# Biases by ScalarE's queue in pieces, once-filled slots for a later expert's down rows, and a reordered start and end of an expert loop

## The chip, the cores and the metric

One core of a Trainium2 chip runs one program. The metric is device time in microseconds of one launch, median of the runs shown. The engines are TensorE (PE), VectorE (DVE), ScalarE (ACT), GpSimd (POOL) and SyncE (SP), which here issues every DMA. Sixteen DMA engines serve the core. Everything is float32.

## What is computed

Two blocks in sequence on 256 tokens of width 1024. The first (two layers of feed-forward, gated mixers, feed-forward) is not touched. The second is an attention layer followed by a mixture of 32 experts, of which each token takes 4:

```python
def moe_ffn(h, w_router, b_router, w_gate_up, b_gate_up, w_down, b_down):
    logits = (h @ w_router).astype(jnp.float32) + b_router.astype(jnp.float32)
    top_val, top_idx = lax.top_k(logits, TOP_K)
    gates = jax.nn.softmax(top_val, axis=-1)
    ...
    def expert_block(args):
        xe, e = args
        gu = xe @ w_gate_up[e] + b_gate_up[e]
        g = jnp.minimum(gu[:, :D_FF_2], SWIGLU_LIMIT)
        u = jnp.clip(gu[:, D_FF_2:], -SWIGLU_LIMIT, SWIGLU_LIMIT)
        act = (u + 1.0) * (g * jax.nn.sigmoid(SWIGLU_ALPHA * g))
        return act @ w_down[e] + b_down[e]
    ...
# the layer returns x + gate2 * y, y the gated sum over a token's experts
```

Per expert, `w_gate_up[e]` is 1024x2048 (8 MB) and `w_down[e]` 1024x1024 (4 MB), so the 32 experts read 384 MB.

## The kernel before

`attend_phase` ends with the router; `experts_phase` follows it and does for each expert at most 64 tokens (CAP). More than 64 would go to `late_experts`, which doesn't run on these inputs.

**Tiles and slots.** An expert has 8 gate-up tiles of 128x2048 and 4 down tiles that hold 256 rows of `w_down`, each 1 MB and one DMA. All loads have a number in order of use: `number(e, j)`. Expert 0's gate-up is 0 to 7; then each turn e has 12: gate-up of e (j = 0 to 7) and the down rows of e - 1 (j = 8 to 11). Numbers run through a cycle of 12 slots (6 of `chip.ring`, 6 of `room.more`). Besides there are EXTRA = 4 slots that are filled once (`room.once`), in words that become free when attention is done. Before, they hold the numbers 12 to 15, that is gate-up tiles 4 to 7 of expert 1. Loads 0 to 11 and those four are in flight or landed when the experts start, the last two issued at the start of `experts_phase`.

**SP** (`turn(e)` of the sync block) issues first the row of biases of e (`bias_row`, 8 KB into one partition, waits until the row before has been broadcast), then the loads. Each load waits on `chip.used`, which PE raises when it has read the tile that was in the slot (`emptied`). All these DMAs stand in SP's one queue.

**POOL** (`spread_bias`) broadcasts the row to 128 partitions when it has landed and when `activate(e - 1)` has read the one before (`gu_read`). A small addition (L2616) stands before the broadcast (L2617).

**PE**, per turn: `gate_up(e)` (L2637; after its fourth tile `turn_back`, L2663, two transposes), `gather(e)` (L2672, picks the tokens of e + 1), `down(e)` (L2653), `turn_hidden(e)` (L2682, transposes), `scatter(e)` (L2692, four products of 64 rows that add the expert's output into four PSUM banks that hold the whole result). Turn 0 has gate-up and gather, then four products with `b_down` (L2719, 32 rows), which set the banks, then `turn_hidden(0)`. Turn 1 is written out, and only it has `add_x` (L2699), which adds x through the identity. Turns 2 to 31 are a loop.

**ACT**, per turn: `take_back` (L2735), `take_gathered` (L2740), `sigmoid` (L2744), `take_hidden` (L2748). **DVE**: selections, `activate` (L2790 to L2806), `take_down` (L2812). At the end ACT copies token block 0 (L2762) and DVE token block 1 (L2835) from PSUM, both after the whole last scatter, and SP stores both (L2500).

Of the kernel before, what the change touches and what calls it, by code (L numbers as in the profile page):

```python
# [11 lines left out]
P = 128  # L12
RING = 6
EXTRA = 4
# [1596 lines left out]

def attend_loads(chip, w_in, w_out):
# [56 lines left out]
def attend_phase(chip, s, spent, routed, room, par, loads, base, n_project, b_down, mod_row, w_gate_up, rows_before):  # L1669
# [26 lines left out]
    with nc.Block() as block:  # L1696
        @block.sync
        def _(sp):
# [29 lines left out]
            for i in range(EXTRA - 1):  # L1728
                sp.dma_start(room.once[i], gate_up_rows(w_gate_up, *divmod(2 * RING + i, KD))).then_inc(chip.once[i], 16)
# [420 lines left out]
        def _(dve):  # L2150
# [290 lines left out]
CAP = 64  # L2441
ACC, GATE_BANK, UP_BANK, Y_BANK, SHARED_BANK = 0, 4, 5, 6, 7
EXPERTS = ("e_bias_row e_bias gu_read g_ready sig gated hidden sel back back_turned back_out gathered xe "
           "turned act ye scat down_bias tables first_rows last_rows")
# [16 lines left out]
LATE_WORDS = 2048 + 256 + 1 + 4 * 1024 + 256 + NE + 1 + 6 * SLOT + P  # L2461
# [19 lines left out]
class LateRoom:  # L2481


    def __init__(self, chip, words):
# [7 lines left out]
        self.places = w.take(P)  # L2492
# [5 lines left out]
def store(chip, sp, routed, out, tt, done):  # L2498

    sp.dma_start(out[0:1, tt * P:tt * P + P, :].rearrange("b p d -> (b p) d"), routed.acc[:, tt, :]).then_inc(done, 16)  # L2500


def experts_phase(chip, s, spent, base, routed, room, gatesT, b_down, w_gate_up, b_gate_up, w_down, out):
# [16 lines left out]

    def once(e, j):

        return number(e, j) - CYCLE if isinstance(e, int) and CYCLE <= number(e, j) < CYCLE + EXTRA else None

    def in_cycle(e, j):

        if isinstance(e, int):
            n = number(e, j)
            turn, p = divmod(n if n < CYCLE else n - EXTRA, CYCLE)
# [26 lines left out]
    def emptied(e, j):  # L2556
# [3 lines left out]
        n = number(e, j) - EXTRA - CYCLE  # L2560
        return base + (n if n < CYCLE else n + EXTRA) + 1
# [3 lines left out]
    with nc.Block() as block:  # L2565
        @block.sync
        def _(sp):
            def bias_row(e):
                reach(sp, s["e_bias"], e)
                sp.dma_start(room.bias_row[0:1, :],  # L2570
                             b_gate_up[0:1, ds1(e), :].rearrange("a e n -> (a e) n")).then_inc(s["e_bias_row"], 16)

            def down_rows(e, k):
                return w_down[0:1, ds1(e), 2 * k * P:2 * k * P + 2 * P, :].rearrange("a e (c p) n -> p (a e c) n", p=P)

            def load(e, j, src):

                if not isinstance(e, int) or number(e, j) >= CYCLE + EXTRA:
# [26 lines left out]
            sp.wait_ge(s["first_rows"], 1)  # L2605
            store(chip, sp, routed, out, 0, chip.stored)
            sp.wait_ge(s["last_rows"], 1)
# [17 lines left out]
        def _(pe):  # L2625
            mm = nc.tensor.matmul

            def gate_up(e, between=None):

                pe.wait_ge(s["xe"], e + 1)  # L2630
                reach(pe, s["gu_read"], e)
                for k in range(G8):
# [53 lines left out]
            def scatter(e):  # L2686
# [15 lines left out]
            def turn(e):  # L2702
                gate_up(e, lambda: turn_back(e))
# [3 lines left out]
                if isinstance(e, int):  # L2707
                    add_x()
                scatter(e)
# [360 lines left out]
```

## Time and profile before

| | us |
|---|---|
| runs: median of 3 (lowest, highest) | 2349.98 (2349.85, 2355.32) |
| the profiled execution | 2348.43 |
| its span, first to last instruction | 2346.8 |
| PE busy | 2238.3 (95%) |
| DVE busy | 1027.9 (44%) |
| ACT busy | 597.7 (25%) |
| POOL busy | 169.7 (7%) |
| experts_phase, about | 1374 to 2346.8 |

The profile is one execution. Its times count from the first instruction. A busy PE isn't PE at its peak: matmuls are pipelined. "DMA share" is the mean busy share of the 16 DMA engines; transfers of one engine overlap a little, so a full stream is shown slightly above 1. PEclk is the granted clock of TensorE as a part of full speed.

### The profile page before, as it was taken

To read this page: it belongs to the slowest core of one execution; us is meant where nothing else is said; L and a number is where in the kernel's file an instruction comes from. 1 tells how busy PE (TensorE), PEld (TensorE's weight loads), DVE (VectorE), ACT (ScalarE), POOL (GpSimd) and SP (SyncE) were. 2 spreads that over 40 slices of the span, in tenths; PEclk is the share of its full clock that TensorE was granted. 3 is DMA by queue.
4 is the path that set the end of the run, shared out by engine and by line. 5 is a ranking of instruction groups with operands and counts; after the bars stand their busy time and mean duration, and the time that the engine had idled before them with its cause. 6 is when DMAs were issued, how large, how long until landed. Compare 5 with 4: busy or idle time off the path is not lost. (4 is left out here: it accounts for less than half of the span.)

```text
span 2346.8 us, 32064 instructions
## 1 busy us (share of the span) xinstructions
PE 2238.3 (95%) x12797; PEld 1401.5 (60%) x12798; DVE 1027.9 (44%) x1492; ACT 597.7 (25%) x808; POOL 169.7 (7%) x194
## 2 busy tenths in 40 slices
PE   7999989999999999999999999999999999999998
PEld 6886875788788777668877554444333333333333
DVE  4563583665565457456658642222222222212221
ACT  4432331543443232243436510000000000000000
POOL 5000020000000002000000001000000000000000
PEclk9999999999999999999999999999999999999999
DMA  8763311686386342168635568999999999999996
GB/s 285 240 245 105 122 60 59 213 285 234 122 282 241 104 162 73 38 199 278 213 133 171 211 264 344 416 418 418 418 418 418 418 418 418 418 418 418 418 418 270
DMA packets 231966, 633.58 MB, mean 270 GB/s; under 512 B 32480, under 2 KB 128752, under 8 KB 199072
## 3 DMA queue, kind: packets, MB, share of 16 engines
q1 hardware_dynamic: 231872, 632.24, 71.2%
q8 instruction: 70, 1.15, 0.2%
q14 instruction: 24, 0.20, 0.0%
HBM read 631.12 MB, written 1.07 MB: 269 GB/s over the span
## 5 line engine op out<-in xcount | busy, mean ns | idle before, releaser
L403 PE MATMUL banks<-ffn_room 128*128 128x512 f32 x1920 | 453.7, 392 | 0.0
L403 PEld LDWEIGHTS banks<-ffn_room 128*128 128x128 f32 x1920 | 357.6, 188 | 72.6
L520 DVE TENSOR_TENSOR ffn_room<-memory,ffn_room 128x2048 fp32r<-128x2048 f32 x124 | 280.9, 2292 | 98.6 <-ACT ffn_room L480 98.6
L2790 DVE TENSOR_TENSOR attend_words<-banks,memory 64x512 f32<-64x512 f32 x64 | 44.2, 690 | 550.4 <-PE banks L2637 550.0
L480 ACT CAST ffn_room<-memory 128x2048 fp32r<-128x2048 f32 x124 | 232.0, 1903 | 68.4 <-PE banks L421 61.8
L421 PE MATMUL banks<-ffn_room 128*128 128x512 f32 x1056 | 248.2, 390 | 0.3
L2637 PE MATMUL banks<-attend_later,attend_words 128*64 128x512 f32 x1000 | 232.7, 600 | 14.7 <-DMA attend_later<-in_w_gate_up 12.2
L2653 PE MATMUL banks<-memory,attend_words 128*64 128x512 f32 x1008 | 223.5, 595 | 0.0
L421 PEld LDWEIGHTS banks<-ffn_room 128*128 128x128 f32 x1056 | 197.7, 188 | 42.7 <-DVE ffn_room L559 2.1
L2637 PE MATMUL banks<-memory,attend_words 128*64 128x512 f32 x776 | 179.9, 599 | 13.1 <-DMA memory<-in_w_gate_up 12.4
L2637 PEld LDWEIGHTS banks<-attend_later,attend_words 128*64 128x64 f32 x1000 | 66.8, 137 | 154.8 <-issue 102.4
L2653 PEld LDWEIGHTS banks<-memory,attend_words 128*64 128x64 f32 x1008 | 69.0, 136 | 128.6 <-issue 119.8
L2672 PEld LDWEIGHTS banks<-attend_words,memory 128*128 128x128 f32 x1056 | 120.5, 192 | 26.0 <-issue 26.0
L2637 PEld LDWEIGHTS banks<-memory,attend_words 128*64 128x64 f32 x776 | 50.6, 136 | 136.6 <-issue 103.1
L2672 PE MATMUL banks<-attend_words,memory 128*128 128x64 f32 x1056 | 124.8, 277 | 0.0
L2740 ACT COPY attend_words<-banks 128x512 f32<-128x512 f32 x33 | 19.4, 587 | 401.1 <-PE banks L2672 401.1
L486 ACT ACTIVATE memory<-banks 128x256 f32<-128x256 f32 x88 | 33.8, 385 | 341.5 <-PE banks L403 319.5
L535 DVE TENSOR_TENSOR memory<-memory,banks 128x256 f32<-128x256 f32 x88 | 36.8, 418 | 175.4 <-ACT memory L486 164.2
L869 PE MATMUL banks<-memory 128*128 128x400 f32 (+1 forms) x256 | 101.1, 549 | 1.2 <-PEq L363 1.2
L2617 POOL PARTITION_BROADCAST memory<-attend_words x32 | 73.7, 2304 | 267.3 <-issue 267.3
L2812 DVE TENSOR_TENSOR attend_words<-banks,kept 128x512 f32<-128x512 f32 x32 | 22.2, 693 | 147.2 <-PE banks L2653 147.2
L865 PE MATMUL banks<-memory 128*128 128x256 f32 x384 | 85.4, 379 | 0.0
(430 smaller groups left out, 2328.9 us busy)
## 6 DMA issues: line engine op xcount, KB each, us to landing
memory<-in_ffn_w SPq DMA_DIRECT2D x132, 1024.0 KB, 7.3
memory<-in_w_down SPq DMA_DIRECT2D x126, 1024.0 KB, 24.6
attend_later<-in_w_gate_up SPq DMA_DIRECT2D x125, 1024.0 KB, 20.7
memory<-in_w_gate_up SPq DMA_DIRECT2D x97, 1024.0 KB, 17.8
attend_words<-in_w_gate_up SPq DMA_DIRECT2D x33, 1024.0 KB, 23.7
memory<-in_w_in SPq DMA_DIRECT2D x32, 1024.0 KB, 6.0
memory<-in_w_ada SPq DMA_DIRECT2D x32, 768.0 KB, 5.3
memory<-in_w_out SPq DMA_DIRECT2D x12, 1024.0 KB, 4.9
```

The costliest lines, as they stand in the source:

```text
L403: m = nc.tensor.matmul(psum[:, GU + tt, :], x_parts[:, xp, k, tt * P:tt * P + P], rows, start=(n == 0), stop=(n == 3 * KD - 1))
L421: return nc.tensor.matmul(psum[:, 2 * tt + h, :], hidden_parts[:, ft % 2, hp, tt, c, :], rows[:, c, h * 512:h * 512 + 512], start=(ft == 0 ...
L480: nc.scalar.copy(split_place(i)[0], chip.ring[:, chip.slot(base + i), :]).then_inc(s["lead"], 1)
L520: tt_op(b, chip.ring[:, chip.slot(base + i), :], a.bitcast(F32), ALU.subtract).then_inc(chip.used, 1)
L535: tt_op(hidden[:, tt, :], gate[:, tt, :], psum[:, GU + tt, FT:2 * FT], ALU.mult)\
L865: m = mm(psum[:, n % 2, c * 256:c * 256 + 256], slots[k // 4][:, k % 4, cc:cc + P], chip.xT[:, k, :], start=(k == 0), stop=(k == KD - 1))
L869: m = mm(psum[:, n % 2, 0:cols], chip.xT[:, k, half * P:half * P + P], slots[k // 4][:, k % 4, :], start=(k == 0), stop=(k == KD - 1))
L2617: nc.gpsimd.partition_broadcast(room.bias, room.bias_row[0:1, :]).then_inc(s["e_bias"], 1)
L2637: m = mm(psum[halves[h], bank, :], room.xeT[:, k, :], rows[:, c0 + h * HALF:c0 + h * HALF + HALF], start=(k == 0), stop=(k == G8 - 1))
L2653: m = mm(psum[halves[h], Y_BANK, :], room.actT[:, k, :], rows[:, c * D_EXPERT + h * HALF:c * D_EXPERT + h * HALF + HALF], start=(k == 0), ...
L2672: m = mm(psum[:, SHARED_BANK, k * CAP:k * CAP + CAP], routed.h2[:, tt, k * P:k * P + P], room.sel[:, tt, :], start=(tt == 0), stop=(tt == ...
L2790: m = tt_op(room.gate[halves[h], :], psum[halves[h], GATE_BANK, :], room.bias[halves[h], h * HALF:h * HALF + HALF], ALU.add)
```

## The change

1. SP issues no rows of biases. ACT does, from its own queue, as a pattern of 16 pieces of 512 B, row e + 1 between `take_back(e)` and `take_gathered(e)`.
2. The once-filled slots hold the numbers 40 to 43 (`APART` = 3), the down rows of expert 2, read in turn 3. Numbers 12 to 39 go through the cycle of 12. Turns 1 to 3 are written out, since the numbering is irregular there.
3. Turn 0 takes the first two gate-up tiles of expert 1 (`AHEAD`) before `turn_hidden(0)`; turn 1 begins with the third. The products with x and with `b_down` stand together before turn 8 (`QUIET`); scatter(1) sets the banks.
4. The last scatter signals after token block 0. ACT and DVE each copy one half of a block, and the store of block 0 can be issued before block 1 is copied.
5. The late rounds are a loop of two instead of being written twice (left out below but for its head).

```diff
-EXTRA = 4
+EXTRA, APART = 4, 3
...
+def down_pair(w_down, e, k):
+
+    return w_down[0:1, ds1(e), 2 * k * P:2 * k * P + 2 * P, :].rearrange("a e (c p) n -> p (a e c) n", p=P)
...
             sp.wait_ge(s["pv"], ALL)
             for i in range(EXTRA - 1):
-                sp.dma_start(room.once[i], gate_up_rows(w_gate_up, *divmod(2 * RING + i, KD))).then_inc(chip.once[i], 16)
+                sp.dma_start(room.once[i].rearrange("p (c n) -> p c n", c=2), down_pair(w_down, APART - 1, i)).then_inc(chip.once[i], 16)
...
+BIAS_PIECES = 16
+AHEAD = 2
...
+    apart = number(APART, G8)
+
     def once(e, j):
 
-        return number(e, j) - CYCLE if isinstance(e, int) and CYCLE <= number(e, j) < CYCLE + EXTRA else None
+        return number(e, j) - apart if isinstance(e, int) and apart <= number(e, j) < apart + EXTRA else None
...
-        n = number(e, j) - EXTRA - CYCLE
-        return base + (n if n < CYCLE else n + EXTRA) + 1
+        n = number(e, j) - CYCLE
+        if n + CYCLE >= apart:
+            n -= EXTRA
+        return base + (n if n < apart else n + EXTRA) + 1
...
-                if not isinstance(e, int) or number(e, j) >= CYCLE + EXTRA:
+                if not isinstance(e, int) or number(e, j) >= CYCLE:
                     sp.wait_ge(chip.used, emptied(e, j))
...
             def turn(e):
-                late = isinstance(e, int) and e == 2
-                if not late:
-                    bias_row(e)
-                for k in range(G8 if isinstance(e, int) and e == 1 else 0, G8):
+                for k in range(D4 if isinstance(e, int) and e == 1 else 0, G8):
                     load(e, k, gate_up_rows(w_gate_up, e, k))
-                if late:
-                    bias_row(e)
+                if isinstance(e, int) and e == APART:
+                    return
                 for k in range(D4):
                     load(e, G8 + k, down_rows(e - 1, k))
 
-            bias_row(0)
-            for n in (CYCLE - 1, CYCLE + EXTRA - 1):
-                load(1, n - G8, gate_up_rows(w_gate_up, 1, n - G8))
-            turn(1)
-            turn(2)
-            with sp.Fori(3, NE) as e:
+            load(1, D4 - 1, gate_up_rows(w_gate_up, 1, D4 - 1))
+            sp.dma_start(room.once[EXTRA - 1].rearrange("p (c n) -> p c n", c=2), down_rows(APART - 1, EXTRA - 1))\
+                .then_inc(chip.once[EXTRA - 1], 16)
+            for e in range(1, APART + 2):
+                turn(e)
+            with sp.Fori(APART + 2, NE) as e:
                 turn(e)
...
-            def scatter(e):
+            def scatter(e, first=False):
...
-                               start=False, stop=True, skip_group_check=True)
+                               start=first, stop=True, skip_group_check=True)
+                    if tt == 0 and isinstance(e, int) and e == NE:
+                        m.then_inc(s["scat_first"], 1)
                 m.then_inc(s["scat"], 1)
 
-            def add_x():
+            def add_x_and_bias():
+                pe.wait_ge(s["down_bias"], 1)
                 for tt in range(NT):
                     for h in range(2):
-                        mm(psum[:, ACC + 2 * tt + h, :], ident, chip.x[:, tt, h * 512:h * 512 + 512],
-                           start=False, stop=True, skip_group_check=True)
+                        c = slice(h * 512, h * 512 + 512)
+                        for rows, cols in ((ident, chip.x[:, tt, c]), (gatesT[0:NE, tt * P:tt * P + P], b_down[0:NE, c])):
+                            mm(psum[:, ACC + 2 * tt + h, :], rows, cols, start=False, stop=True, skip_group_check=True)
 
             def turn(e):
-                gate_up(e, lambda: turn_back(e))
+                gate_up(e, range(AHEAD if isinstance(e, int) and e == 1 else 0, G8), lambda: turn_back(e))
                 gather(e)
                 down(e, G8)
                 turn_hidden(e)
-                if isinstance(e, int):
-                    add_x()
-                scatter(e)
+                scatter(e, isinstance(e, int) and e == 1)
...
             gather(0)
-            pe.wait_ge(s["down_bias"], 1)
-            for tt in range(NT):
-                for h in range(2):
-                    c = slice(h * 512, h * 512 + 512)
-                    mm(psum[:, ACC + 2 * tt + h, :], gatesT[0:NE, tt * P:tt * P + P], b_down[0:NE, c], start=True, stop=True)
+            gate_up(1, range(AHEAD))
             turn_hidden(0)
-            turn(1)
-            with pe.Fori(2, NE) as e:
+            for e in range(1, APART + 1):
+                turn(e)
+            with pe.Fori(APART + 1, QUIET) as e:
+                turn(e)
+            add_x_and_bias()
+            with pe.Fori(QUIET, NE) as e:
                 turn(e)
...
+            def bias_row(e):
+                reach(act, s["e_bias"], e)
+                act.dma_start(room.bias_row[0:1, :].rearrange("p (a n) -> p a n", a=BIAS_PIECES),
+                              b_gate_up[0:1, ds1(e), :].rearrange("a e (k n) -> (a e) k n", k=BIAS_PIECES))\
+                    .then_inc(s["e_bias_row"], 16)
...
+            bias_row(0)
             take_gathered(-1)
+            bias_row(1)
             take_gathered(0)
             sigmoid(0)
             take_hidden(0)
-            with act.Fori(1, NE) as e:
+            with act.Fori(1, NE - 1) as e:
                 take_back(e)
+                bias_row(e + 1)
                 take_gathered(e)
...
             take_back(NE)
+            act.wait_ge(s["scat_first"], 1)
+            copy(routed.acc[:, 0, 0:512], psum[:, 0, :]).then_inc(s["first_rows"], 1)
             act.wait_ge(s["scat"], NE)
-            copy(routed.acc[:, 0, :], psum[:, 0:2, :].rearrange("p b n -> p (b n)")).then_inc(s["first_rows"], 1)
+            copy(routed.acc[:, 1, 0:512], psum[:, 2, :]).then_inc(s["last_rows"], 1)
...
-                for first_place in (CAP, CAP + P):
-                    late_round(chip, s, routed, room, w_gate_up, b_gate_up, w_down, e, first_place, gate2_row, out)
+                with nc.Fori(0, 2) as half:
+                    late_round(chip, s, routed, room, w_gate_up, b_gate_up, w_down, e, half, gate2_row, out)
```

DVE's two last copies change in the same way, to the halves 512 to 1024 of blocks 0 and 1.

## Rows read from the trace of the kernel before

**Rows 1.** The page, slices of 58.7 us: busy tenths of the 16 DMA engines.

```profile
DMA  8763311686386342168635568999999999999996
```

**Rows 2.** Timeline of POOL: start, duration (us), engine, line, operation, idle before and releaser.

```profile
1481.03 0.35 POOL L2616 TENSOR_TENSOR attend_words<-memory 128x1 f32<-128x1 f32 x1 [16.30 <-DVE attend_words L2795]
...
1564.80 0.35 POOL L2616 TENSOR_TENSOR attend_words<-memory 128x1 f32<-128x1 f32 x1 [16.70 <-DVE attend_words L2795]
...
1623.60 0.19 POOL L2616 TENSOR_TENSOR attend_words<-memory 128x1 f32<-128x1 f32 x1 [19.64 <-DMA attend_words<-in_b_gate_up]
...
2293.36 0.19 POOL L2616 TENSOR_TENSOR attend_words<-memory 128x1 f32<-128x1 f32 x1 [19.54 <-DMA attend_words<-in_b_gate_up]
```

**Rows 3.** Timeline of PE, last gate-up tiles of two late turns.

```profile
1732.24 1.94 PE L2637 MATMUL banks<-attend_words 128*64 128x512 f32 x8 [0.55 <-DMA attend_words<-in_w_gate_up]
1734.73 1.94 PE L2637 MATMUL banks<-memory,attend_words 128*64 128x512 f32 x8 [0.56 <-DMA memory<-in_w_gate_up]
...
2313.22 1.94 PE L2637 MATMUL banks<-memory,attend_words 128*64 128x512 f32 x8 [0.56 <-DMA memory<-in_w_gate_up]
```

**Rows 4.** Timeline of SP's issues, turns 0 to 2 (L2583 loads, L2570 biases).

```profile
1386.74 2.13 SPq L2583 DMA_DIRECT2D memory<-in_w_down  x4
...
1411.67 0.29 SPq L2570 DMA_DIRECT2D attend_words<-in_b_gate_up  x1
1424.26 5.52 SPq L2583 DMA_DIRECT2D memory<-in_w_down  x4
1430.85 0.27 SPq L2570 DMA_DIRECT2D attend_words<-in_b_gate_up  x1
```

**Rows 5.** Waits of SP, 1370 to 1450 us: total, times, longest.

```profile
SPq L2570 <- POOL memory L2617: 12.3, 2, 11.6
```

**Rows 6.** Timeline of PE, turns 0 and 1 (eight records are a gate-up tile).

```profile
1379.06 10.53 PE L2637 MATMUL banks<-memory,attend_words 128*64 128x512 f32 x48 [0.68 <-ACT attend_words L2740]
...
1396.67 5.53 PE L2719 MATMUL banks<-attend_later,attend_words 32*128 32x512 f32 x8
...
1418.57 3.79 PE L2672 MATMUL banks<-attend_words,memory 128*128 128x64 f32 x32
...
1429.80 3.61 PE L2699 MATMUL banks<-memory 128*128 128x512 f32 x8
```

**Rows 7.** Windows: length, busy (count) of PE, PEld, DVE, ACT, POOL; PEclk, DMA share, GB/s.

```profile
1392.00:1416.00 24.00, 24.00 (x106) 10.60 (x104) 5.87 (x12) 3.47 (x5) 2.65 (x2) 0.86 1.02 415
1416.00:1440.00 24.00, 24.00 (x120) 10.59 (x118) 6.80 (x13) 1.71 (x3) 2.66 (x2) 1.00 0.64 242
...
1398.00:1405.00 7.00, 7.00 (x16) 2.49 (x16) 2.34 (x6) 1.89 (x3) 0.00 (x0) 0.53 1.02 424
```

**Rows 8.** Windows at the end of the stream, same columns.

```profile
2322.00:2324.00 2.00, 2.00 (x12) 0.57 (x9) 0.00 (x0) 0.00 (x0) 0.00 (x0) 1.00 0.57 227
2324.00:2326.00 2.00, 2.00 (x12) 0.61 (x9) 0.06 (x1) 0.00 (x0) 0.00 (x0) 1.00 0.08 33
...
2332.00:2334.00 2.00, 2.00 (x12) 0.71 (x10) 0.00 (x0) 0.00 (x0) 0.00 (x0) 1.00 0.03 12
```

**Rows 9.** The page, DMA queues: packets, MB, share of 16 engines.

```profile
q8 instruction: 70, 1.15, 0.2%
```

**Rows 10.** Timeline of all engines in turn 31.

```profile
2302.84 2.30 POOL L2617 PARTITION_BROADCAST memory<-attend_words  x1 [9.28 <-issue]
...
2305.83 0.37 ACT L2735 COPY attend_words<-banks 128x256 f32<-128x256 f32 x1 [9.06 <-PE banks L2663]
```

**Rows 11.** Timeline of all engines at the end.

```profile
2336.11 0.69 DVE L2812 TENSOR_TENSOR attend_words<-banks,kept 128x512 f32<-128x512 f32 x1 [8.97 <-PE banks L2653]
...
2336.86 1.99 PE L2692 MATMUL banks<-attend_words 64*128 64x512 f32 x8 [0.80 <-DVE attend_words L2812]
...
2338.89 1.01 ACT L2762 COPY kept<-banks 128x1024 f32<-128x1024 f32 x1 [9.44 <-PE banks L2692]
2338.89 1.23 DVE L2835 COPY kept<-banks 128x1024 f32<-128x1024 f32 x1 [2.09 <-PE banks L2692]
2339.93 0.83 SPq L2500 DMA_DIRECT2D out<-kept  x2
```

More of the change, by code:

```diff
@@ L1666, with attend_phase @@
 PIECES = ((0, P), (P, WIDE))
-def attend_phase(chip, s, spent, routed, room, par, loads, base, n_project, b_down, mod_row, w_gate_up, rows_before):
+def attend_phase(chip, s, spent, routed, room, par, loads, base, n_project, b_down, mod_row, w_gate_up, w_down, rows_before):
     nc, D, KD, NT = chip.nc, chip.D, chip.KD, chip.NT
@@ L2491, in __init__ @@
         self.selT = w.take(256).rearrange("p (t n) -> p t n", t=2)
-        self.places = w.take(P)
+        self.places = w.take(2 * P).rearrange("p (a n) -> p a n", a=2)
         self.xeT, self.actT = chip.xT[:, :, 0:P], chip.xT[:, :, P:2 * P]
@@ L2528, in in_cycle @@
             n = number(e, j)
-            turn, p = divmod(n if n < CYCLE else n - EXTRA, CYCLE)
+            turn, p = divmod(n if n < apart else n - EXTRA, CYCLE)
             return p, 0, turn
@@ L2626, in _, with gate_up @@
             mm = nc.tensor.matmul
-            def gate_up(e, between=None):
+            def gate_up(e, tiles, between=None):
                 pe.wait_ge(s["xe"], e + 1)
                 reach(pe, s["gu_read"], e)
-                for k in range(G8):
+                for k in tiles:
                     pe.wait_ge(full(e, k), filled(e, k))
@@ L2759, in _ @@
                 take_hidden(e)
+            take_back(LAST)
+            take_gathered(LAST)
+            sigmoid(LAST)
+            take_hidden(LAST)
             take_back(NE)
+            act.wait_ge(s["scat_first"], 1)
+            copy(routed.acc[:, 0, 0:512], psum[:, 0, :]).then_inc(s["first_rows"], 1)
             act.wait_ge(s["scat"], NE)
-            copy(routed.acc[:, 0, :], psum[:, 0:2, :].rearrange("p b n -> p (b n)")).then_inc(s["first_rows"], 1)
+            copy(routed.acc[:, 1, 0:512], psum[:, 2, :]).then_inc(s["last_rows"], 1)
         @block.vector
@@ L2833, in _, with late_round @@
             take_down(NE, taken(NE, D4))
+            dve.wait_ge(s["scat_first"], 1)
+            nc.vector.tensor_copy(routed.acc[:, 0, 512:1024], psum[:, 1, :]).then_inc(s["first_rows"], 1)
             dve.wait_ge(s["scat"], NE)
-            nc.vector.tensor_copy(routed.acc[:, 1, :], psum[:, 2:4, :].rearrange("p b n -> p (b n)")).then_inc(s["last_rows"], 1)
+            nc.vector.tensor_copy(routed.acc[:, 1, 512:1024], psum[:, 3, :]).then_inc(s["last_rows"], 1)
 LATE = ("chain l_gate l_added l_stored l_sel l_gathered l_xeT l_bias_row l_bias l_rows l_gu l_summed l_capped l_sig l_gated l_hidden l_turned "
         "l_actT l_down l_ye l_selT l_scat")
-def late_round(chip, s, routed, room, w_gate_up, b_gate_up, w_down, e, first_place, gate2_row, out):
+def late_round(chip, s, routed, room, w_gate_up, b_gate_up, w_down, e, half, gate2_row, out):
     nc, D, KD, NT = chip.nc, chip.D, chip.KD, chip.NT
@@ L2932, in _ @@
             chain = Chain(dve, s["chain"])
-            chain(ts(room.places, routed.iota, float(first_place), None, ALU.add))
+            for i in range(2):
+                chain(ts(room.places[:, i, :], routed.iota, float(CAP + i * P), None, ALU.add))
             for tt in range(NT):
-                m = ts(room.sel[:, tt, :], room.places, routed.place[:, tt, ds1(e)],
+                m = ts(room.sel[:, tt, :], room.places[:, ds1(half), :].rearrange("p a n -> p (a n)"), routed.place[:, tt, ds1(e)],
                        routed.chosen[:, tt, ds1(e)], ALU.is_equal, ALU.mult)
@@ L2982, in second_half @@
             room = AttendRoom(chip, parts, later, words, routed)
-            attend_phase(chip, s_attend, s_first.span(), routed, room, par, loads, base, n_project, b_down, mod_row, w_gate_up, rows_before)
+            attend_phase(chip, s_attend, s_first.span(), routed, room, par, loads, base, n_project, b_down, mod_row, w_gate_up, w_down, rows_before)
             experts_phase(chip, s_first, s_late.span(), base + n_project + N_OUT, routed, ExpertRoom(chip, words, room), room.gatesT, room.b_down,
```

18 lines of the change are left out of this document (7 added, 11 removed).

## The prediction, made before the changed kernel ran

> **What bounds the kernel now.** I read the page's slices first: from slice 25 on, some 1410 us to the end, the DMA row stands at 9 without a break [rows 1]. That stretch is the 32 experts, 12 loads of 1 MB each. PE is about as busy, so the next view must tell which of the two sets the pace.
>
> The timeline of POOL has one mark per expert: the small addition in front of the broadcast, released when `activate` has read the banks. Between 1481.03 and 1564.80 the mark comes three times in 83.77 us, 27.9 us a turn; between 1623.60 and 2293.36 it comes 22 times in 669.76 us, 30.44 us a turn [rows 2]. PE's timeline says why: in the second stretch the last gate-up tiles start 2.49 us apart and each has waited for a DMA, against 10.53 / 6 = 1.75 us a tile where nothing is awaited [rows 3, 6]. So PE needs 27.9 us a turn and DMA 30.4. PE eats up the lead of 16 loads, and from about 1600 us it runs at DMA's pace. From the mark at 1564.80 to the one at 2293.36 are 24 turns; at 27.92 each the latter would stand at 2234.9. PE has 58 us to spare, and what DMA gains up to that amount is gained at the end.
>
> So the end is: when the stream starts, plus its work, plus its idle time, plus the tail behind the last gate-up tile. Each has a row.
>
> **Start.** SP issues the first load of the long stream at 1386.74 [rows 4], right behind the row of biases of expert 1, for which it had waited up to 11.6 us on the broadcast of row 0, at L2570 [rows 5]. Yet that load's slot was free when PE had done tile 0: 1379.06 + 1.75 = 1380.8 [rows 6].
>
> **Idle.** In 1416 to 1440 the DMA share is 0.64 where a full stream shows 1.02 [rows 7]: 0.38 x 24 = 9.1 us of idle. The reason is in the order: loads 12 to 15 (expert 1, tiles 4 to 7) lie in the once-filled slots and free nothing, so between tile 11 and the first down tile of expert 0 no slot comes free, and SP, which issued a row of biases at 1411.67, issues its next load at 1424.26 [rows 4].
>
> **One engine late.** At the end the share falls to 0.57 in 2322 to 2324, then stands at 0.08, 33 GB/s, and ends in 2332 to 2334 with 0.03 [rows 8]. 1/16 is 0.0625: one DMA engine works on alone. Fifteen stop at 2322 + 2 x (0.57 - 0.06) / (1.02 - 0.06) = 2323.1, the last near 2333.0, 9.9 us later. A load counts as landed with its slowest engine, so PE has been paced by that one. What it has more of is the 8 KB row of biases: 31 in the stream. A tile is 1 MB over 16 engines in 2.49 us, so 8 KB on a single one cost 2.49 / 8 = 0.31 us.
>
> **The change, part by part.** Expert turns are 30.44 = 8 x 2.49 + 0.31 + 4 down tiles, so a down tile is 2.55.
>
> (1) *Rows by ScalarE, in 16 pieces of 512 B.* SP no longer waits for a broadcast: the stream starts at 1380.8, **5.9 us** earlier. In the stream the row leaves the late engine. Two of the 31 rows (experts 2 and 3, issued 1411.67 and 1430.85) fall into idle time and cost nothing now; 29 x 0.31 = 9.0 us are on the path, which the 9.9 us of lag bear out. The 16 pieces aren't free: no row shows 512 B packets between those of another queue. From below they cost 8 KB / 16, 0.02 us on each engine; from above, the instruction queue gives 70 packets of 16 KB at 0.2% of 16 engines, 1.07 us each against 0.62 by the loads' pace [rows 9], so 0.45 us for a packet of another queue. I take 0.05, near the bytes, because the instruction packets partly hit cold engines: 29 x 0.26 = **7.5 us**. ScalarE's issue sits between `take_back` and `take_gathered`. It waits for the broadcast of e; that ends at 2302.84 + 2.30 = 2305.14 and the copy of `take_back` starts at 2305.83 [rows 10], and the next gather, whose result ScalarE copies, comes only behind the last gate-up tile of 2313.22 [rows 3], some 9 us later. Behind the waiting issue are the gathered copy, the sigmoid and the hidden copy; with 9 us of cover this is worth nothing. Without cover every microsecond would be PE's, which has 2.5 a turn.
>
> The Trainium skill, "DMA: Bandwidth & Descriptors", section "Why a DMA increments its semaphore by 16 and not by 1", says that a DMA of SP or ACT runs on the largest k up to 16 that divides the slowest dimension of both patterns, on the lowest-numbered engines, and that a contiguous row sprays if software splits it; the trace agrees that one engine carries the row and that it is the same one each time (9.9 us of lag could not add up otherwise). The same page, "Issuing engines are not separate DMA queues", speaks against half of this part: another issuing engine saves only sequencer time. By that rule the queue alone would be worth the 5.9 us of SP's wait and the splitting the rest.
>
> (2) *Once-filled slots for expert 2's down rows.* The number of loads behind the start stays: 16 lie there beforehand, and up to the last gate-up tile 360 follow. Four are now gate-up instead of down: -0.2 us. What changes is the releases: each of tiles 0 to 39 frees a slot at once. I follow both clocks. DMA, from 1381.9 (data start about 1 us behind the issue), has done 8 loads by 1402; load 20 needs tile 8 read, and with (3) that is 1399.2. It has done 8 more by 1422; load 28 needs tile 16 read: 1418.2. Load 32: DMA 1432, slot 1427.5. Load 44 (slot of 28): DMA 1452, slot 1446. Margins are 1.6 us or more after that 1 us, so the idle time goes: **9.1 us**.
>
> (3) *Two tiles of expert 1 in turn 0, and `add_x` and the bias product moved to turn 8.* The 8 matmuls of 32 rows at L2719 took 5.53 us in turn 0, half of it at a granted clock of 0.5, that is 1.2 GHz instead of 2.4, and `add_x` at L2699 3.6 us in turn 1 [rows 6, 7]. By themselves they save nothing at the end, PE not being the bound; they are the margins of (2): without the two tiles, tile 8 would wait for the sigmoid and its slot would be free about 3.5 us later, an idle time of 2. In turn 8 the same 16 matmuls cost PE 7 to 9 us once, hidden by its 58.
>
> (4) *Last sum by token block.* The eight records of `scatter` take 1.99 us from 2336.86, then ACT copies 1.01 and DVE 1.23 us, and SP issues at 2339.93 [rows 11]. After: block 0 is copied in halves of 512 columns (0.69 us for 128x512 on DVE [rows 11], ACT no longer) from 2337.9 on and stored under the rest; block 1 is out at 2338.9 + 0.7 = 2339.6 instead of 2340.3. Gain 0.6 (copies alone) to 1.3 (the first store's transfer too); I take **0.9**.
>
> Late rounds don't run; their new loop costs nothing. Three unrolled turns instead of one mean more cold code on PE; turn 1, unrolled today, shows no stall.
>
> **Sum.** 5.9 + 7.5 + 0.2 + 9.1 + 0.9 = 23.6. The profiled execution took 2348.43 (span 2346.8), so 2324.8; it lies 1.55 below the median of the runs, 2349.98, hence 2326.4. PE check: gate-up of expert 1, now done at 1418.6 [rows 6], is done some 6 us earlier (5.5 of L2719, and the wait for the sigmoid filled), 1412.6; 30 turns of 27.92 and 9 us for turn 8 give 2259 for the last tile, and DMA brings it at 2313.2 - 22.7 (the sum without the tail) = 2290.5. DMA stays the bound to the end.
>
> **Rivals.**
> A. *The row isn't what makes the engine late, or the pieces cost as much as they free.* Only start, idle and tail pay: 15.9 to 16.1, giving 2334. For it: nobody sees engine numbers in these views. Against: 9.0 worked out, 9.9 read. 12%.
> B. *Releases in turn 0 and 1 come later than I count*, through half clock on tiles 8 and 9 (1.75 us more each, the clock stood at 0.53 in 1398 to 1405 [rows 7]). Then DMA idles up to 3.5 us: 2330. 12%.
> C. *The idle time comes back elsewhere* (a queue waits for something that I overlook, or PE gets near its bound): only a third of the gain, 2342 to 2349. 5%.
> D. *Slower: a second ring breaks the stream.* If each row on ACT's queue makes every engine pause for x, the loss is 29x. The whole gain, with the row's 0.31 freed, is 5.9 + 9.0 + 0.2 + 9.1 + 0.9 = 25.1, so it turns at x = 0.87 us; at 1.2 the time is 2360. The nearest row, 0.45, lies below. 4%.
> My forecast has 67%, for itself from 2322 to 2331. All cases but C and D are faster by more than 0.3% (about 7 us, what a measurement of this kernel can tell from no change): 0.92 with part of C; same 0.04; slower 0.04. Range: pieces at their bytes, tail at 1.3 and the 9.9 us of lag in full give 25.8 and 2324; I go to 2321 for the spread of runs, and up to 2335 to take in A and B.
>
> **What would show it.** The first down-row load issued by SP near 1381 and no hole in DMA before 1460; the share at the end falling from full to nothing without a stretch of one sixteenth; marks of POOL 30.1 to 30.2 us apart in the late turns; two stores issued about 0.9 us apart. Marks 30.4 apart would break (1), a hole in 1402 to 1446 would break (2). If the marks come 27.9 apart to the end, PE is the bound and my clocks are wrong.

## The result, and the profile after

| | before | after |
|---|---|---|
| median of the runs, us | 2349.91 | 2333.98 |
| lowest, highest | 2349.4, 2355.32 | 2332.8, 2335.07 |
| profiled execution, its span | 2348.43, 2346.8 | 2332.8, 2331.0 |

The ratio is 0.9929, with a 95% interval of 0.9917 to 0.9941: faster by 16 us. That is 7.6 us above the forecast of 2326.4, and inside the range only because its upper end had been moved to 2335 to take in rivals A and B. The first thing to look at is DMA's queues on the page of the changed kernel (packets, MB, share of 16 engines). ACT's queue is q10:

```profile
q1 hardware_dynamic: 231808, 631.98, 71.8%
q8 instruction: 73, 1.20, 0.2%
q10 hardware_dynamic: 64, 0.26, 0.0%
```

32 rows of 8 KB are 0.26 MB, and 64 packets are two for each row. Sixteen pieces would be at least sixteen packets a row, so the pieces, which lie one behind the other on both sides, were moved as one. I read the two as one packet of data and one for the semaphore: spread8, wide_row and four_rows have 1024, 994 and 256 packets, which fits as many packets again as data packets. The marks of POOL (start, duration, engine, line, operation, idle before) say what that is worth; [rows 2] has their counterpart:

```profile
1585.44 0.35 POOL L2621 TENSOR_TENSOR attend_words<-memory 128x1 f32<-128x1 f32 x1 [15.59 <-DVE attend_words L2816]
...
1621.80 0.36 POOL L2621 TENSOR_TENSOR attend_words<-memory 128x1 f32<-128x1 f32 x1 [23.80 <-DVE attend_words L2816]
...
1819.84 0.35 POOL L2621 TENSOR_TENSOR attend_words<-memory 128x1 f32<-128x1 f32 x1 [19.43 <-DVE attend_words L2816]
...
2276.30 0.35 POOL L2621 TENSOR_TENSOR attend_words<-memory 128x1 f32<-128x1 f32 x1 [19.89 <-DVE attend_words L2816]
```

From 1819.84 to 2276.30 are 15 turns of 30.43 us, as in [rows 2]. The step of 36.36 us at 1621.80 is a PE-bound turn of 27.92 plus 8.44 for the products in front of turn 8. The windows (length, busy of PE, PEld, DVE, ACT, POOL, then PEclk, DMA share, GB/s) show the hole of [rows 7] gone from its place and the late engine of [rows 8] still there:

```profile
1392.00:1416.00 24.00, 23.32 (x130) 10.83 (x126) 7.26 (x14) 3.47 (x5) 2.48 (x2) 1.00 1.02 414
1416.00:1440.00 24.00, 23.79 (x121) 9.44 (x121) 5.18 (x11) 2.09 (x4) 2.48 (x2) 1.00 1.02 415
```

```profile
2312.00:2314.00 2.00, 2.00 (x13) 0.61 (x10) 0.16 (x1) 0.00 (x0) 0.00 (x0) 1.00 0.31 125
2314.00:2316.00 2.00, 1.79 (x12) 0.83 (x10) 1.04 (x3) 0.59 (x1) 0.00 (x0) 1.00 0.07 27
...
2320.00:2322.00 2.00, 2.00 (x12) 0.65 (x10) 0.00 (x0) 0.00 (x0) 0.00 (x0) 1.00 0.03 10
```

A smaller hole stands further on. SP issues four down tiles until 1470.8 and its next load only at 1485.96 (timeline), and the windows of this profile and of the second one of the same kernel (after_again) show DMA waiting:

```profile
1465.27 5.52 SPq L2591 DMA_DIRECT2D memory<-in_w_down  x4
1485.96 2.06 SPq L2591 DMA_DIRECT2D memory<-in_w_gate_up  x2
```

```profile
1484.00:1488.00 4.00, 4.00 (x20) 1.30 (x20) 0.00 (x0) 0.00 (x0) 1.69 (x1) 1.00 0.79 279
```

```profile
1484.00:1488.00 4.00, 4.00 (x20) 1.34 (x20) 0.00 (x0) 0.00 (x0) 2.31 (x1) 1.00 0.42 128
```

That is 0.23 x 4 = 0.9 us of idle, and 0.60 x 4 = 2.4 us in the second. PE reads the once-filled tiles 40 to 43 there (1474 to 1481), and they free no slot, just as tiles 12 to 15 did before. So the hole did not go: 9.1 us became 0.9 to 2.4, 70 us later.

SP's first issues of the experts, and the end (timelines), beside [rows 4] and [rows 11]:

```profile
1375.62 0.34 SPq L2591 DMA_DIRECT2D memory<-in_w_gate_up  x1
1376.01 0.43 SPq L2602 DMA_DIRECT2D attend_later<-in_w_down  x1
1382.94 5.48 SPq L2591 DMA_DIRECT2D memory<-in_w_gate_up  x4
```

```profile
2301.11 1.94 PE L2641 MATMUL banks<-memory,attend_words 128*64 128x512 f32 x8 [0.55 <-DMA memory<-in_w_gate_up]
...
2324.76 1.99 PE L2696 MATMUL banks<-attend_words 64*128 64x512 f32 x8 [0.80 <-DVE attend_words L2833]
```

The span can now be cut at four marks. The first load that SP issues in the experts: 1374.02 before, 1375.62 after, 1.6 us *lost*. From there to the first load of the stream: 12.72 against 7.32, 5.4 won. From there to the last gate-up tile: 1386.74 to 2313.22 is 926.5, 1382.94 to 2301.11 is 918.2, 8.3 won. From that tile to the end of the span: 33.6 against 29.9, 3.7 won. The sum is 15.8, the difference of the spans.

### The profile page after: what moved, and what is told of

It is laid out like the page before. It is cut to its first block and busy times, and to the rows that moved or that the text cites. A ratio compares the mean times of both kernels' runs of the same rounds, so it can differ in the third digit from the quotient of the medians.

```text
span 2331.0 us, 31950 instructions
## 1 busy us (share of the span) xinstructions
PE 2234.3 (96%) x12797; PEld 1402.8 (60%) x12798; DVE 1054.4 (45%) x1493; ACT 598.0 (26%) x809; POOL 174.4 (7%) x194
## 5 line engine op out<-in xcount | busy, mean ns | idle before, releaser
L2641 PE MATMUL banks<-attend_later,attend_words 128*64 128x512 f32 x960 | 221.5, 597 | 7.7 <-DMA attend_later<-in_w_gate_up 7.0
```

What stands on the lines that cost most here:

```text
L2641: m = mm(psum[halves[h], bank, :], room.xeT[:, k, :], rows[:, c0 + h * HALF:c0 + h * HALF + HALF], start=(k == 0), stop=(k == G8 - 1))
```

## The experiments

Times are medians, ratios are to the kernel before run beside it. The changed kernel again gives the scale for the others.

**after_again.** The changed kernel, no edit.

> The changed kernel as it is, beside the three others on the same chip. Both theories: 2334, within 2 us, and 16 us under the kernel before. Late marks of POOL 30.4 us apart, and one DMA engine working on alone for about 8 us at the end of the stream. It also tells whether the 1.9 us by which its experts began later than before's (1375.6 against 1373.7) is there each time.

2335.85 us, ratio 0.9943 (0.9929 to 0.9956). Its experts begin at 1374.38, against 1375.62 in the first profile; the other profiles with the change lie between 1375 and 1379, and before_four, below, whose front is the old one, begins at 1376.06 where the kernel before began at 1374.02. So the 1.6 us lost in front of them can't be put down to the change. Parts in the profile of one kernel repeat to about 2 us (this stream took 920.3, the first 918.2), and 1.5 us of that is the second hole, 2.4 against 0.9. The marks repeat much better: 30.43 in both, and 30.41 to 30.44 in every other profile below that has the change and the row as one packet.

Only no_rows, spread16 and spread8 ran beside this one. The others are set against it by their ratios to the kernel before, and where a difference is near the width of the intervals (some 3 us either way), I go by the parts of the profiles.

Another part varies. From the start of the first tile of expert 0 to the first load of the stream are 1.98 us in seven profiles with the change, and 3.67 in four, no_rows, wide_row, ahead0 and sums_early, where PE's granted clock was 0.54 in the mean, near its lower level of 1.2 GHz (first the changed kernel, then ahead0):

```profile
1380.96:1382.94 1.98, 1.98 (x10) 0.77 (x12) 1.72 (x4) 0.00 (x0) 0.00 (x0) 1.00 0.73 296
```

```profile
1380.71:1384.38 3.67, 3.67 (x10) 1.17 (x12) 1.71 (x4) 0.00 (x0) 0.00 (x0) 0.54 0.38 156
```

These four lose 1.7 us at the start of the stream, and none of their edits touches PE up to there.

**no_rows.** Is it the rows that make an engine late?

```diff
 def bias_row(e):
+    if not isinstance(e, int) or e > 0:
+        return
     reach(act, s["e_bias"], e)
...
-pool.wait_ge(s["e_bias_row"], (e + 1) * 16)
+pool.wait_ge(s["e_bias_row"], 16)
```

> Left out: the loads of the rows of biases of experts 1 to 31; row 0 is used for all of them, so the output differs. Theory one (the row is a single packet of 8 KB on always the same DMA engine, 0.31 us a turn): late marks 30.1 us apart instead of 30.43, no stretch of a sixteenth at the end of the stream, 8 to 10 us less, about 2325. Rival (that engine is late for another reason, such as instruction fetches or being slower by itself): marks stay 30.4 apart, the stretch stays, 2334.

2327.74 us, ratio 0.9902 (0.9887 to 0.9917). Marks of POOL and the windows at the end of the stream:

```profile
1851.56 0.35 POOL L2621 TENSOR_TENSOR attend_words<-memory 128x1 f32<-128x1 f32 x1 [17.83 <-DVE attend_words L2818]
...
2273.20 0.35 POOL L2621 TENSOR_TENSOR attend_words<-memory 128x1 f32<-128x1 f32 x1 [18.79 <-DVE attend_words L2818]
```

```profile
2314.00:2316.00 2.00, 2.00 (x12) 0.61 (x10) 0.00 (x0) 0.24 (x1) 0.00 (x0) 1.00 0.96 383
2316.00:2318.00 2.00, 2.00 (x12) 0.67 (x10) 0.00 (x0) 0.00 (x0) 0.00 (x0) 1.00 0.39 158
2318.00:2320.00 2.00, 2.00 (x12) 0.72 (x10) 0.00 (x0) 0.00 (x0) 0.00 (x0) 1.00 0.00 0
```

Fourteen turns in 421.64 are 30.12 each, 0.31 under 30.43, and all engines stop together. The cost of theory one holds: the row takes 0.31 us a turn, and nothing else makes an engine late. A perfect cure is worth about 8 us.

**spread16 and spread8.** Pieces that can't be joined, because each DMA takes every second one:

```diff
-act.dma_start(room.bias_row[0:1, :].rearrange("p (a n) -> p a n", a=BIAS_PIECES),
-              b_gate_up[0:1, ds1(e), :].rearrange("a e (k n) -> (a e) k n", k=BIAS_PIECES))
+for i in range(2):
+    act.dma_start(room.bias_row[0:1, :].rearrange("p (a b n) -> p a b n", b=2, a=16)[:, :, i, :],
+                  b_gate_up[0:1, ds1(e), :].rearrange("a e (k b n) -> (a e) k b n", b=2, k=16)[:, :, i, :])
```

(a = k = 8 in spread8.)

> The row as two DMAs of 16 pieces of 64 words each, with gaps between the pieces so that they cannot be joined into one. Theory one: 32 packets of 256 B a row over the engines, the stretch of a sixteenth goes, marks 30.1 to 30.2 apart, 2325 to 2328. Rival (the engine is late for another reason): 2334. If small packets of a second queue break the stream by 0.3 us or more on each engine, nothing is gained or it is slower: 2334 to 2340.

> The row as two DMAs of 8 pieces of 128 words each, again with gaps. Theory one: 16 packets of 512 B on eight engines (two each, 1 KB instead of 8 KB on the busiest), marks 30.1 to 30.2 apart, 2325 to 2328, and not slower than the 256 B pieces. Rival: 2334.

2337.23 (0.9945, 0.9931 to 0.9959) and 2337.95 (0.9945, 0.9931 to 0.9958): no gain. The pieces are real this time, as ACT's queue on the page of spread16 shows, 64 packets a row (by the reading above, half of them data):

```profile
q10 hardware_dynamic: 2048, 0.27, 0.1%
```

Yet one engine is late again (spread16, windows at the end), and the marks are 30.61 us apart in spread16 (1852.04 to 2280.58, 14 turns) and 30.55 in spread8:

```profile
2314.00:2316.00 2.00, 2.00 (x12) 0.69 (x10) 0.00 (x0) 0.00 (x0) 0.00 (x0) 1.00 0.24 98
2318.00:2320.00 2.00, 1.79 (x12) 0.96 (x12) 1.20 (x3) 0.60 (x1) 0.00 (x0) 1.00 0.07 27
2324.00:2326.00 2.00, 2.00 (x12) 0.62 (x10) 0.00 (x0) 0.00 (x0) 0.00 (x0) 1.00 0.04 14
```

So theory one was half a theory. The row costs one engine 0.31 us, but not because that engine fetches all of it: with the pieces spread, that cost doesn't fall, it rises to 0.49 and 0.43, and the engine left over at the end is still a single one (share 0.06 to 0.07). What all pieces still share is their destination, partition 0.

**wide_row.** The same 16 packets with another destination:

```diff
-act.dma_start(room.bias_row[0:1, :].rearrange("p (a n) -> p a n", a=BIAS_PIECES),
-              b_gate_up[0:1, ds1(e), :].rearrange("a e (k n) -> (a e) k n", k=BIAS_PIECES))
+act.dma_start(room.bias_row[0:P:8, 0:P],
+              b_gate_up[0:1, ds1(e), :].rearrange("a e (k n) -> (a e k) n", k=16))
```

> From the changed kernel: rows 1 to 31 go in 16 pieces of 512 B to 16 partitions, eight apart, instead of into partition 0 (changes the computation: the broadcast goes on reading partition 0, whose first 128 words are those of the row and the rest those of row 0). Theory after the pieces into one partition had left one engine late (marks 30.54 and 30.60): what is scarce is the way into the partition, so the engine that fills that partition's group for the tiles is slowed whoever brings the 8 KB. Then here marks 30.12 to 30.2 apart, no stretch of a sixteenth at the end, 2327 to 2329. Rival: any row of ACT's queue holds one engine up, by its descriptors or its semaphore: marks 30.4 to 30.6, one engine late, 2336 to 2338.

2329.32 us, ratio 0.9905 (0.9889 to 0.992). Marks from 1850.43 to 2272.83, 14 turns of 30.17, and no engine works on alone:

```profile
2314.00:2316.00 2.00, 2.00 (x12) 0.58 (x10) 0.00 (x0) 0.00 (x0) 0.00 (x0) 1.00 0.65 262
2316.00:2318.00 2.00, 2.00 (x12) 0.71 (x10) 0.00 (x0) 0.00 (x0) 0.00 (x0) 1.00 0.16 66
2318.00:2320.00 2.00, 2.00 (x12) 0.57 (x8) 0.00 (x0) 0.00 (x0) 0.00 (x0) 1.00 0.00 0
```

The queue, the bytes and the number of pieces a row (16, as in spread8) are those of kernels that stayed slow; the destination differs, and the cost goes from 0.43 down to 0.05. The rival (any row of ACT's queue) falls. One thing differs besides: spread8 takes two DMAs a row and wide_row one. That wasn't tried by itself, but the changed kernel, with one DMA a row into partition 0, paid 0.31. The broadcast still reads partition 0, so behind the first row this kernel leaves out 15 of 16 parts of each.

**four_rows.** A version that computes the reference with that knowledge:

```diff
-act.dma_start(room.bias_row[0:1, :].rearrange("p (a n) -> p a n", a=BIAS_PIECES),
-              b_gate_up[0:1, ds1(e), :].rearrange("a e (k n) -> (a e) k n", k=BIAS_PIECES))
+act.dma_start(room.bias_row[0:P:32, 0:HALF],
+              b_gate_up[0:1, ds1(e), :].rearrange("a e (k n) -> (a e k) n", k=4))
...
-nc.gpsimd.tensor_tensor(room.idle, chip.eps[:, 0:1], chip.eps[:, 1:2], ALU.add)
-nc.gpsimd.partition_broadcast(room.bias, room.bias_row[0:1, :]).then_inc(s["e_bias"], 1)
+nc.gpsimd.tensor_tensor(room.idle[0:16], chip.eps[0:16, 0:1], chip.eps[0:16, 1:2], ALU.add)
+for i in range(4):
+    m = nc.gpsimd.partition_broadcast(room.bias[:, i * HALF:i * HALF + HALF], room.bias_row[32 * i:32 * i + 1, 0:HALF])
+m.then_inc(s["e_bias"], 1)
```

> From the changed kernel, computing the same: each row of biases goes as four parts of 2 KB to partitions 0, 32, 64 and 96, and POOL broadcasts each part from there. Theory (the way into the partitions 0 to 7 is what the row uses up): four groups of partitions take 2 KB each instead of one taking 8, 0.08 us a turn on the late ones: marks 30.2 apart, the stretch of a sixteenth at the end about a quarter as long (2 to 3 us), 2329 to 2331 where the changed kernel gives 2335 to 2336. Risk: four broadcasts in a row keep POOL longer than the turn allows, ACT then waits with the next row, and the marks come later than 30.4 apart. Rival (any row of ACT's queue costs an engine 0.3 us): 2335 to 2337.

2329.17 us, ratio 0.9906 (0.9891 to 0.9921), against 0.9943 (0.9929 to 0.9956) and 0.9929 (0.9917 to 0.9941), the two ratios of the changed kernel: 5 to 9 us less, and its interval just meets the second of these. The profiles put it at the lower end: the span is 4.4 and 5.4 us shorter, and the marks below give 29 x 0.15 = 4.4. POOL's timeline and the end of the stream:

```profile
2271.97 0.26 POOL L2621 TENSOR_TENSOR attend_words<-memory 16x1 f32<-16x1 f32 x1 [21.12 <-DVE attend_words L2818]
2278.57 2.87 POOL L2623 PARTITION_BROADCAST memory<-attend_words  x4 [6.33 <-issue]
```

```profile
2312.00:2314.00 2.00, 2.00 (x12) 0.82 (x12) 0.00 (x0) 0.38 (x1) 0.00 (x0) 1.00 0.65 262
2314.00:2316.00 2.00, 2.00 (x12) 0.64 (x10) 0.00 (x0) 0.00 (x0) 0.00 (x0) 1.00 0.29 117
2316.00:2318.00 2.00, 2.00 (x12) 0.65 (x10) 0.00 (x0) 0.00 (x0) 0.00 (x0) 1.00 0.02 6
```

Several engines are late now: 0.29 of 16 is four to five. They are so by some 2 us, and since even in no_rows the share takes about 2 us to fall, neither number is sharp. Four broadcasts take 2.87 us together, one took 2.30 [rows 10], so the feared cost isn't there. The marks are 30.28 apart (1847.99 to 2271.97, 14 turns): 0.16 us a turn where I had expected 0.08. That is twice what a quarter of the bytes would cost each of four engines. It is what half of them would cost, 0.31 / 2 = 0.155 by my estimate, as if the four destinations fell on two engines; wide_row's 0.05 is likewise nearer to an eighth of 0.31 (0.04) than to a sixteenth (0.02). The share of 0.29 speaks for more than two late engines. No run separates the two accounts, and it stays open which engines the four destinations slow.

**before_four.** Was that the kernel before's trouble too? The same edit of POOL and of the DMA's shape in the kernel before, SP issuing as it did.

> From the kernel before, computing the same: SP issues the row of biases where it did, but as four parts of 2 KB to partitions 0, 32, 64 and 96, and POOL broadcasts each from there; nothing of the change is in it. Theory (before's late DMA engine was late by the rows and by nothing else): marks 30.2 to 30.3 apart instead of 30.44, start and hole of the stream as they were, a stretch with few engines at the end of 2 to 3 us instead of 9.9, 6 to 7 us less than the kernel before: 2344 to 2346. Rival (in SP's own queue the row cost something else, such as a break between loads): no gain, 2350 to 2352.

2347.26 us, ratio 0.9982 (0.9973 to 0.9991), 4 us where 6 to 7 were expected. The marks are 30.28 apart and the late stretch short (share 0.34 in 2330 to 2332, 0.17 in the next 2 us, then none), so the mechanism holds. The marks are worth 29 x 0.16 = 4.6 us, where I had reckoned with 0.08 a turn for the parts: these 2.3 us are the shortfall, or most of it. The hole was also larger in that profile: the share in 1412 to 1436 is 0.66, it stays under a full stream until 1448, and it comes to 10.8 us in all against 9.1.

**sp_rows.** Part 1 undone: the lines of `bias_row` back in SP's `turn`, and gone from ACT.

> From the changed kernel with one part undone: the rows of biases issued by SP in front of a turn's loads, as in the kernel before. Theory: the stream starts 5.7 us later (behind the broadcast of row 0) and nothing else changes, since the row costs its engine the same in either queue: 2341 to 2342 where the changed kernel gives 2336. Rival: the hole in the DMA stream of 1416 to 1440 would have swallowed the later start, so that the two parts overlap and less than 2 us are lost: 2336 to 2338.

2345.53 us, ratio 0.9973 (0.9963 to 0.9983): 7 us behind the changed kernel by the ratios, more than I had expected. SP's timeline:

```profile
1376.95 0.36 SPq L2596 DMA_DIRECT2D memory<-in_w_gate_up  x1
...
1389.28 0.24 SPq L2586 DMA_DIRECT2D attend_words<-in_b_gate_up  x1
1389.57 1.98 SPq L2596 DMA_DIRECT2D memory<-in_w_gate_up  x4
...
1426.32 2.08 SPq L2596 DMA_DIRECT2D attend_later<-in_w_down  x2
1444.80 0.25 SPq L2586 DMA_DIRECT2D attend_words<-in_b_gate_up  x1
1445.09 0.82 SPq L2596 DMA_DIRECT2D attend_later<-in_w_gate_up  x2
```

From its first load to the stream are 12.6 us, 5.3 more than 7.3. Then the row of expert 3 waits in SP until 1444.80 for a broadcast, with the loads of turn 3 behind it, and another row does so near 1467. The windows have the price:

```profile
1440.00:1448.00 8.00, 8.00 (x52) 4.32 (x47) 2.69 (x5) 0.00 (x0) 2.30 (x1) 1.00 0.41 157
1464.00:1472.00 8.00, 8.00 (x38) 2.54 (x36) 0.00 (x0) 0.38 (x1) 2.30 (x1) 1.00 0.81 307
```

(1.02 - 0.41) x 8 + (1.02 - 0.81) x 8 = 6.6 us of idle. The changed kernel's own hole near 1484 isn't there in return, so 4.2 to 5.7 us are left, and the stream (1389.57 to 2312.90, 923.3) is 3.0 to 5.2 longer. So ACT's queue protects the stream from each wait, not from the first alone, once the slots come free early.

**once_gate_up.** Part 2 undone: `apart = CYCLE`, gate-up tiles 4 to 7 of expert 1 in the once-filled slots.

> From the changed kernel with one part undone: the once-filled slots hold gate-up tiles 4 to 7 of expert 1 again. Theory: load 28 waits for the first down tile to be read, some 6 to 7 us after DMA has finished load 27; a hole in the DMA share between turn 1's gate-up and its down, 2342 to 2343. Rival: the two tiles in turn 0 and the moved products had already closed the hole: within 2 us of 2336.

2339.5 us, ratio 0.9953 (0.9939 to 0.9967). The intervals overlap with the changed kernel's; the profile decides:

```profile
1412.00:1424.00 12.00, 12.00 (x74) 6.26 (x70) 4.94 (x8) 1.11 (x2) 0.18 (x1) 1.00 0.51 188
```

The hole is there, 0.51 x 12 = 6.1 us as worked out, but the stream (1383.43 to 2307.14, 923.7) is only 3.4 to 5.5 us longer than the changed kernel's two (920.3, 918.2). The second hole makes up the difference: near 1484 this kernel has none (share 1.02 in 1480 to 1500), where the changed one has 2.4 and 0.9, and 6.1 less these is 3.7 and 5.2. So the once-filled slots for a later expert were worth about 4.5 us and not 6.

**ahead0.** `AHEAD = 0`.

> From the changed kernel with one part undone: no tile of expert 1 in turn 0, so PE waits there for the sigmoid. Theory: tile 8 is read some 4 us later, DMA idles 1.5 to 2 us between loads 19 and 20 and nowhere else, 1 to 2 us lost, 2337 to 2338. Rival: PE's spare time covers it, same as the changed kernel.

2339.85 us, ratio 0.9951 (0.9937 to 0.9965); here too the profile tells more than the ratio. PE's timeline, and the window:

```profile
1404.36 1.09 PE L2686 MATMUL banks<-memory,attend_words 128*128 128x128 f32 x4 [4.28 <-DVE attend_words L2827]
1405.38 4.98 PE L2641 MATMUL banks<-attend_later,attend_words 128*64 128x512 f32 x16
```

```profile
1404.00:1412.00 8.00, 7.64 (x30) 2.89 (x32) 1.06 (x5) 0.59 (x1) 1.85 (x1) 0.74 0.64 226
```

PE stands 4.28 us, and behind the pause its granted clock falls, 0.74 in the mean of these 8 us, that is partly 1.2 GHz: two tiles take 4.98 us instead of 3.65. The hole is 0.38 x 8 = 3.0 us, not 1.5 to 2. I had expected no other. But the second hole is larger too:

```profile
1488.00:1496.00 8.00, 7.79 (x38) 2.71 (x38) 1.46 (x5) 0.59 (x1) 2.30 (x1) 1.00 0.69 261
```

0.33 x 8 = 2.6 us. With 5.6 us of idle against 0.9 and 2.4 the stream should be 4.7 and 3.2 us longer; it is 5.6 and 3.5 (923.8). The rest of the run's loss is the 1.7 us of the first tile's clock.

**sums_early.** The products behind turn 1 instead of in front of turn 8.

> From the changed kernel with one part undone in place: the products with x and with b_down stand behind turn 1 instead of in front of turn 8. Theory: turn 2 begins 8.4 us later, slot of load 32 comes free near 1438 while DMA has finished load 31 near 1434.5, so the stream has a hole of 4 to 5 us there; 3 to 5 us lost, 2339 to 2341. Rival: PE has tens of microseconds to spare over the whole stream, so the place of 8 us of its work doesn't matter: same as the changed kernel.

2342.92 us, ratio 0.9961 (0.9948 to 0.9975), 4 us behind the changed kernel by the ratios, the intervals overlapping a little (0.9948 to 0.9956). The windows:

```profile
1436.00:1444.00 8.00, 8.00 (x29) 2.53 (x30) 0.00 (x0) 0.00 (x0) 0.00 (x0) 1.00 0.55 199
1492.00:1500.00 8.00, 7.79 (x39) 2.80 (x38) 1.65 (x5) 0.60 (x1) 2.30 (x1) 1.00 0.39 121
```

0.47 x 8 = 3.8 us of hole where it was worked out, a little under the 4 to 5 expected. A second one that wasn't expected follows, 0.63 x 8 = 5.0 us: PE, held up by the 8.4 us of products, comes later to the first tile behind the once-filled ones. Together 8.8 us of idle, 7.9 and 6.4 more than the changed kernel, and the stream (926.9) is 8.7 and 6.6 longer. The rival, that 58 us of spare time hide 8 us of work wherever they stand, is wrong; in front of turn 8 they hide it.

**late_twice.** `for half in range(2)` in place of the loop.

> From the changed kernel with one part undone: the late rounds, which don't run, are written out twice in the program instead of in a loop of two. Theory: the end of the program jumps over more code and waits for a further fetch of instructions, so the span ends about 3.1 us after the last store has landed instead of 0.8: 2338. Rival: code that isn't run costs nothing: 2336, and the end of the changed kernel differs from before's for another reason.

2337.6 us, ratio 0.9941 (0.9928 to 0.9955), no difference that the times can tell from 0.9943. In the profile the last scatter starts at 2326.82 and the span ends at 2335.6, 8.8 us later; the changed kernel takes 6.24 (2324.76 to 2331.0), 6.33 in its second profile, and the nine other profiles with the loop lie between 6.24 and 6.34; the kernel before takes 9.94 [rows 11]. SP's waits at the end of late_twice (total, times, longest):

```profile
SPq L2993 <- DVEq L2993: 2.7, 1, 2.7
SPq L2993 <- DMA out<-kept: 0.9, 1, 0.9
```

In the changed kernel the wait for the stores is the longest at this place, 0.9 us; here SP waits 2.7 us more for DVE's sequencer. That the written-out rounds cost 2.5 us at the end is shown. That it is a fetch of instructions is not: DMA is at 0.00 from 2333 on, and a small transfer comes only at 2335.8, behind the last instruction.

## Why the prediction was right, and where it failed

The result lies in the range, but the mechanism of the forecast held only in part. 7.5 of the 23.6 us didn't come, and that 2334 fits rival A so well is in part luck: the tail gave 2.8 us more than its term, and the front, the start and the stream together 3.1 less.

*Start, 5.9.* Right: 5.4 in the profiles, and 5.3 lost when it is undone (sp_rows). Where the first tile ran at a clock of 0.54, as in four of the profiles, 3.7 are left.

*Rows in pieces, 7.5.* Wrong, and as large as the whole miss. The step that failed is "in the stream the row leaves the late engine". Its price was right: 0.31 us a turn, measured as 30.43 against 30.12. But the 16 pieces went out as one packet, so nothing changed. The time is that of rival A (12%, 2334), its reasons aren't: the row does make the engine late (no_rows), and what pieces cost didn't come into it, since there were none. I had taken the shape in the source for the shape on the wire. Of the Trainium skill I had used "DMA: Bandwidth & Descriptors", section "Why a DMA increments its semaphore by 16 and not by 1". It goes by the slowest dimension "as the instruction carries it", and the 64 packets show that this instruction didn't carry the 16. And had they gone out, the gain would still have been missed, as spread16 and spread8 show (30.61 and 30.55). The reasoning behind the number, that the late engine is late because it alone carries the row, was wrong; wide_row puts the cost at the destination partitions. The 0.05 taken for 16 pieces is what wide_row measured, but nothing on record had shown it, and it holds only with the pieces in 16 partitions. The same page's table of specifications has the 16 engines on 16 ports into SBUF, eight partitions per engine by convention. No run here shows ports. The single late engine of partition 0 is in line with such a division; four_rows fits an even one only in part, since its four destinations cost 0.16 a turn where a quarter of 0.31 would be 0.08.

*Down-row split, 0.2.* Too small to see.

*Idle, 9.1.* Right in the main: the hole left 1416 to 1440, and the stream became 8.3 and 6.2 us shorter in the two profiles. The term was too large by what came back near 1484, 0.9 and 2.4 us. The prediction followed the two clocks up to load 44 and stopped there. Load 56 waits for tile 44, because tiles 40 to 43 free nothing, and by the same clocks DMA is ready for it at 1432 + 20 x 2.5 = 1482, while tile 44 is read two turns after tile 20, at 1427.5 + 2 x 27.92 = 1483.3. That margin is below zero. Rows 2 and 3, which were free in the old hole and now cost 0.31 each, take 0.6 more.

*Margins of 1.6 us or more.* Borne out up to load 44 by ahead0 and sums_early, which each go below them and open a hole of 3.0 and 3.8 us; past load 44 there was no margin, and the same two runs have 2.6 and 5.0 us of idle there. ahead0's first hole was mis-sized, since the pause also cost the clock. Rival B didn't come: in the first profile the clock stayed at 1.00 in 1392 to 1416, where before it had been 0.86 [rows 7]. In the second it was 0.93, and DMA still showed a full 1.02.

*Tail, 0.9.* From the last scatter to the end 3.7 us went, not 0.9. late_twice gives 2.5 of them to the late rounds, of which I wrote that their loop costs nothing; it didn't cost, it saved, at a place that I hadn't followed. The term was right for the stores alone: the remaining 1.2 are left for them, at the upper end of my 0.6 to 1.3.

*PE isn't the bound.* Right: marks of 27.92 us up to turn 15, then 30.43. The turn of 36.36 has the 8.4 us forecast as 7 to 9.

*Front.* The experts began 1.6 us later. The kernels with the change begin anywhere from 1374.38 to 1378.54 and before_four, without it, at 1376.06, so a cost of the change can't be told from this variation.

## What to carry to other kernels

Where a stream of loads runs without a pause, look at how it ends: a share of one sixteenth at its end is an engine that has set the pace for the whole of it. Then count packets per queue before believing in a split, and spread a small transfer over its destination partitions, not only over its pieces. And where DMA is the bound, PE's spare time is no cover in the first turns, as long as the slot of the next load comes free only with a tile that PE reads. Buffers that are filled once can leave a gap where they are read, since they free no slot there, so follow both clocks past that point.

## What of the hardware was not expected

The cost a turn of the same 8 KB, by the marks less 30.12: 0.31 as one packet into partition 0; 0.43 as 16 of 512 B and 0.49 as 32 of 256 B into partition 0; 0.16 as four of 2 KB into partitions 0, 32, 64 and 96; 0.05 as 16 of 512 B into partitions eight apart. Behind a pause of 4.28 us on PE its granted clock was 0.74 in the mean of 8 us. In four of twelve profiles with the change the granted clock was 0.54 during the first tile of the experts, and the stream began 1.7 us later. With the late rounds written out twice the end of the span was 2.5 us longer, with no load or store left to wait for. The best kernel of this study is four_rows, 2329.17 us beside 2351.55 of the kernel before.
